# A two-layer encoder on one core: fewer, longer rotation operations on GpSimd, and new orders in the opening, the dense layer and the attention head loop

## The reference, cut to what matters

```python
mod = silu(c) @ ada_w + ada_b                      # per layer: sh1, sc1, g1, sh2, sc2, g2
# layer 0
h = modulate(rmsnorm(x, n1), sh1, sc1)
q, k, v, g = split(h @ w_in)                       # 1024, 1024, 2048, 2048 columns
q, k = axial_rope(q), axial_rope(k)                # 4 heads of 256: each half is rotated
x = x + g1 * ((silu(g) * groupnorm(retention(q, k, v))) @ w_out)
h = modulate(rmsnorm(x, n2), sh2, sc2)
x = x + g2 * ((silu(h @ w_gate) * (h @ w_up)) @ w_down)          # dense, 2816 wide
# layer 1
q, k, v = split(modulate(rmsnorm(x, n1), sh1, sc1) @ w_qkv)      # 8 heads, 2 kv heads of 128
q, k = axial_rope(rmsnorm(q)), axial_rope(rmsnorm(k))
x = x + g1 * (softmax(q k^T * scale) v @ w_out)
x = x + g2 * moe_top2_of_8(modulate(rmsnorm(x, n2), sh2, sc2))   # experts 3584 wide
out = modulate(rmsnorm(x, final_norm_g), fsh, fsc)

def rope_1d(x, pos):                               # on one half of a head
    x1, x2 = split(x, 2)
    return concat(x1 * cos - x2 * sin, x1 * sin + x2 * cos)
```

## Time and profile before

| | |
|---|---|
| median of 3 runs | 1586.56 us (1585.43 to 1588.83) |
| the profiled execution's own time | 1589.74 us |
| its span | 1587.9 us |
| instructions | 20528 |
| the chain that ended last, by engine | PE 82%, DVE 10%, ACT 3%, DMA 3%, issue 2% |
| DVE, ACT, POOL busy | 1335.5, 982.5, 198.1 us |
| HBM read | 502.12 MB, 321 GB/s over the span |

### The profile page before, as it was taken

One profiled execution on the slowest core, in us unless ns is written; L12 is line 12 of the kernel. 1 busy time (PEld: TensorE's weight loads), 2 busy tenths in 40 slices (PEclk: granted clock), 3 DMA queues, 4 the chain that ended last, 5 costly groups with the idle time before them and its releaser, 6 DMA issues.

```text
span 1587.9 us, 20528 instructions
## 1 busy us (share of the span) xinstructions
PE 1531.4 (96%) x6818; PEld 1228.9 (77%) x6818; DVE 1335.5 (84%) x1071; ACT 982.5 (62%) x811; POOL 198.1 (12%) x188
## 2 busy tenths in 40 slices
PE   6999998899999799999999999999999999999997
PEld 6777676677777588778888888888888888888885
DVE  6799878877778779998888988988988888888898
ACT  4554434343446555677777767777776777777674
POOL 0499700000020011001001001000000000000320
PEclk9999999999999999999999999999999999999999
DMA  9989735788874179999999999999999999999993
GB/s 342 380 287 350 274 105 201 272 300 298 295 249 166 46 260 344 391 346 369 375 361 367 379 358 363 386 352 365 385 353 367 381 369 352 381 369 352 390 394 141
DMA packets 238896, 508.70 MB, mean 320 GB/s; under 512 B 15494, under 2 KB 38150, under 8 KB 238728
## 3 DMA queue, kind: packets, MB, share of 16 engines
q1 hardware_dynamic: 233824, 491.52, 85.6%
q0 software_dynamic: 4448, 14.55, 2.5%
q10 hardware_dynamic: 584, 2.11, 0.3%
HBM read 502.12 MB, written 7.87 MB: 321 GB/s over the span
## 4 chain that ended last, share of the span: by engine, by line
PE 82%; DVE 10%; ACT 3%; DMA 3%; issue 2%; SPq 0%; DVEq 0%; ACTq 0%
PE bank L1969 25%; PE bank L1970 25%; PE bank L1971 25%; PE bank L2388 2%; DVE lo L1212 1%; DVE lo L1719 1%; DVE hs L1292 1%; DMA stage<-in_l_moe_w_gate 1%; PE bank L1947 1%; PE bank L2075 1%; DVE ada_acc L1224 1%; DVE lo L1609 1%; PE bank L2257 1%; ACT hi L739 0%; DMA stage<-in_l_moe_w_up 0%
## 5 line engine op out<-in xcount | busy, mean ns | idle before, releaser
L1719 DVE TENSOR_TENSOR lo<-stage,hi 128x2048 fp32r<-128x2048 f32 x168 | 388.2, 2319 | 39.6 <-ACT hi L1070 38.8
L1070 ACT CAST hi<-stage 128x2048 fp32r<-128x2048 f32 x168 | 321.3, 1914 | 107.7 <-DMA stage<-in_l_moe_w_up 86.5
L1970 PE MATMUL bank<-lo,hg_hi 128*128 128x512 f32 x896 | 353.7, 395 | 0.0
L739 ACT CAST hi<-stage 128x2048 fp32r<-128x2048 f32 x69 | 131.6, 1910 | 130.8 <-PE bank L1971 103.7
L1970 PEld LDWEIGHTS bank<-lo,hg_hi 128*128 128x128 f32 x896 | 168.9, 189 | 36.8
L1212 DVE TENSOR_TENSOR lo<-stage,hi 128x2048 fp32r<-128x2048 f32 x69 | 159.2, 2311 | 30.5 <-ACT hi L739 24.7
L1719 DVE TENSOR_TENSOR lo<-stage,hi_h 128x2048 fp32r<-128x2048 f32 x56 | 128.3, 2292 | 66.2 <-ACT hi_h L1070 66.2
L1969 PE MATMUL bank<-hi,hg_hi 128*128 128x512 f32 x452 | 178.9, 396 | 0.3 <-issue 0.2
L1971 PE MATMUL bank<-hi,hg_lo 128*128 128x512 f32 x452 | 179.0, 396 | 0.0
L1970 PE MATMUL bank<-lo,eaT_hi 128*128 128x512 f32 x448 | 177.4, 396 | 0.0
L1969 PE MATMUL bank<-hi,hT_hi 128*128 128x512 f32 x400 | 165.8, 415 | 8.5 <-DVE hT_lo L1267 3.4
(11 more groups left out here) (354 smaller groups left out, 2789.1 us busy)
## 6 DMA issues: line engine op xcount, KB each, us to landing
stage<-in_l_moe_w_gate SPq DMA_DIRECT2D x224, 512.0 KB, 5.0
stage<-in_l_moe_w_up SPq DMA_DIRECT2D x224, 512.0 KB, 5.2
stage<-in_l_moe_w_down SPq DMA_DIRECT2D x224, 512.0 KB, 4.9
ada_w<-in_l_ada_w SPq DMA_DIRECT2D x40, 1024.0 KB, 5.5
stage<-in_l_ret_w_in SPq DMA_DIRECT2D x48, 512.0 KB, 6.9
stage<-in_l_ffn_w_gate SPq DMA_DIRECT2D x22, 512.0 KB, 7.9
stage<-in_l_ffn_w_up SPq DMA_DIRECT2D x22, 512.0 KB, 8.7
stage<-in_l_ffn_w_down SPq DMA_DIRECT2D x22, 512.0 KB, 6.5
```

What stands on the lines that cost most here:

```text
L739: nc.scalar.copy(hi_of(b), stage[:, b % RING, :]).then_inc(hi_done, 1)
L1070: nc.scalar.copy(hi_e(b), stage[:, b % RING, :]).then_inc(hi_done, 1)
L1719: nc.vector.tensor_tensor(lo[:, b % RING, :], stage[:, b % RING, :], hi_e(b).bitcast(F32), ALU.subtract).then_inc(lo_done, 1)
L1970: mm(dst_ap, a_hi, w_lo, start=False, stop=False)
```

## The change

Four parts, all in the order of work or in the shape of operations; the sums that are computed stay the same.

1. **Rotation.** The loop over the two halves `f` is folded into the operands: 48 operations of 256 elements for 96 of 128.
2. **Opening.** The first unit is loaded, cast and split in two halves, each with its own semaphore, and DVE makes its `lo` ahead of `columns_pre(0)`. `low` of unit 3 moves ahead of `columns_pre(1)`.
3. **Dense layer.** SP loads a chunk's units ahead of a half of ada weights; each slot on DVE takes the second half of one ada product and the first of the next; PE's `ada_sum` comes one chunk later; `fin(6)` moves in between the first `low` and `f_mul` of the first chunk; `scale(2)` moves ahead.
4. **Attention.** The ada product A_AT-1 moves out of the head loop, ahead of and into the QKV units; its sum comes after the third turn of queries. The heads' values alternate between banks 7 and 3 (the last in 4), with `a_values(h)` waiting for `o_low` of h-2 and not h-1. In ACT's loop `soft(h+2)` comes directly behind `pT_take(h)`, the root of the second query group comes earlier with its table switched ahead (`warm[:, 5:6]`), and the last two splits of output weights (`high_o(3)`, `low_o(2)`, `low_o(3)`) move to the end of the loop.

The core of the diff:

```diff
-                    for f in range(2):
-                        co = cst[:, C_RC + (t * 2 + f) * 64:...].unsqueeze(1).to_broadcast([P, 2, 64])
-                        ...
-                        rotate(v[:, :, f, 0, :], v[:, :, f, 1, :], co, si, ("p (h i) -> p h i", dict(h=2)),
-                               [ropet[:, i, 0:128] for i in range(3)], False)
+                    co, si = (cst[:, c0 + t * 128:c0 + (t + 1) * 128].rearrange("p (f i) -> p f i", f=2).unsqueeze(1)
+                              .to_broadcast([P, 2, 2, 64]) for c0 in (C_RC, C_RS))
+                    rotate(v[:, :, :, 0, :], v[:, :, :, 1, :], co, si, ("p (h f i) -> p h f i", dict(h=2, f=2)),
+                           [ropet[:, i, :] for i in range(3)], False)
 ...
# opening, SP and ACT
-            load_in(0)
+            first = stage[:, 0, :].rearrange("p (k n) -> p k n", k=4)
+            sp.dma_start(first[:, 0:2, :], w_in_v[:, 0:2, 0:CB]).then_inc(w_first, 16)
+            sp.sem_inc(w_load[0], 16)
+            sp.dma_start(first[:, 2:4, :], w_in_v[:, 2:4, 0:CB]).then_inc(w_load[0], 16)
-            high(U_RET)
+            act.wait_ge(w_first, 16)
+            nc.scalar.copy(hi[:, 0, 0:UW // 2], stage[:, 0, 0:UW // 2]).then_inc(hi_half, 1)
+            act.wait_ge(w_load[0], 32)
+            nc.scalar.copy(hi[:, 0, UW // 2:UW], stage[:, 0, UW // 2:UW]).then_inc(hi_done, 1)
# dense, SP (load_dense: two gate/up units and one down unit)
+            load_dense(0, 0)
+            load_ada(A_FF, 0, l1_ada_w, l1_ada_b, 0)
+            load_dense(0, 1)
+            load_ada(A_FF, 1, l1_ada_w, l1_ada_b, 0)
+            load_ada(A_FF + 1, 0, l1_ada_w, l1_ada_b, AC)
# dense, DVE
+            def ada_slot(it, q):
+                ada(A_FF + q - 1, 1, it * 2)
+                ada(A_FF + q, 0, it * 2)
+            f_units(0, 0, between=lambda: fin(6))
+            fin(7)
+            ada(A_FF, 0)
+            f_units(0, 1)
+            ada_slot(0, 1)
# dense, PE
             f_down(U_FF + 4, 0, 0, True, False)
-            ada_sum(A_FF)
             f_turn(1)
-            f_chunk(U_FF + 5, 0, 2, False, A_FF + 1)
+            f_chunk(U_FF + 5, 0, 2, False, A_FF)
 ...
             f_down(U_QKV - 2, 0, N_FF - 2, False, False, between=lambda: f_turn(N_FF - 1))
+            ada_sum(A_AT - 2)
# attention, ACT
+            ada_take(A_AT - 1, mod_at((A_AT - 1 - A_L1) * AC))
+            nc.scalar.activation(warm[:, 5:6], eps, ACT.Sqrt)
+            act.wait_ge(w_used, RING + U_QKV + 6)
+            qkv_squares(2)
             qkv_copy(2)
             for h in range(AH):
                 pT_take(h)
+                if h == 0:
+                    head_roots(2)
+                if h + 2 < AH:
+                    soft(h + 2)
 ...
# attention, PE
+O_BANK = (7, 3, 7, 3, 7, 3, 7, 4)
                 pe.wait_ge(at_pT, h + 1)
-                if h:
-                    pe.wait_ge(o_lo, h)
+                if h >= 2:
+                    pe.wait_ge(o_lo, h - 1)
```

More of the change, by code:

```diff
@@ L1329, in _ @@
             pre(0, range(1, KT))
+            dve.wait_ge(hi_half, 1)
+            nc.vector.tensor_tensor(lo[:, 0, 0:UW // 2], stage[:, 0, 0:UW // 2], hi[:, 0, 0:UW // 2].bitcast(F32), ALU.subtract)
+            dve.wait_ge(hi_done, 1)
+            nc.vector.tensor_tensor(lo[:, 0, UW // 2:UW], stage[:, 0, UW // 2:UW], hi[:, 0, UW // 2:UW].bitcast(F32),
+                                    ALU.subtract).then_inc(lo_done, 1)
             columns_pre(0)
@@ L1342, in _ @@
             pre(1, range(2, 8))
+            low(U_RET + 3)
             columns_pre(1)
@@ L1346, in _ @@
                 low_pre(1, k)
-            for u in range(3, 6):
+            for u in range(4, 6):
                 low(U_RET + u)
@@ L1497, in f_low_act, with f_units @@
                                         part[:, :, :].bitcast(F32), ALU.subtract).then_inc(f_lo, 1)
-            def f_units(it, q):
+            def f_units(it, q, between=None):
                 b = U_FF + 2 + 3 * q
@@ L1503, in f_units @@
                 low(b, it * 6)
+                if between is not None:
+                    between()
                 f_mul(cc - 1)
@@ L1507, in f_units @@
                 low(b + 2, it * 6)
-            def f_pair(it):
+            def ada_slot(it, q):
[6 more added lines that the diff above has]
+            ada_slot(0, 1)
+            last = (N_FF - 1) // 2 - 1
+            with dve.Fori(1, last) as it:
                 for q in range(2):
                     f_units(it, q)
-                    for half in range(2):
-                        ada(A_FF + q, half, it * 2)
-            f_units(0, 0)
-            fin(7)
-            for half in range(2):
-                ada(A_FF, half)
-            f_units(0, 1)
-            for half in range(2):
-                ada(A_FF + 1, half)
-            last = (N_FF - 1) // 2 - 1
-            with dve.Fori(1, last) as it:
-                f_pair(it)
+                    ada_slot(it, q)
             f_units(last, 0)
-            for half in range(2):
-                ada(A_AT - 2, half)
+            ada_slot(last, 0)
+            scale(2, A_L1 + 4)
             f_units(last, 1)
-            scale(2, A_L1 + 4)
+            ada(A_AT - 2, 1)
             low(U_QKV - 1)
@@ L1551, in _ @@
                 low_T(2, (t,))
-            low(U_QKV + 2)
-            low(U_QKV + 3)
             def ada_step(c, k):
@@ L1610, in low_o @@
                                         ALU.subtract).then_inc(lo_done, 1)
+            low(U_QKV + 2)
+            for k in range(2):
+                ada_step(A_AT - 1, k)
+            low(U_QKV + 3)
+            for k in range(2, 5):
+                ada_step(A_AT - 1, k)
             link(head_rope(AH, AKV, ktab, TT))
@@ L1619, in _ @@
             low(U_QKV + 5)
+            for k in range(5, KT):
+                ada_step(A_AT - 1, k)
             head_rope(0, 2, qtab, 2 * TT).then_inc(arope, 1)
@@ L2291, in _ @@
             aq_turn(2)
+            ada_sum(A_AT - 1)
             qkv_half(5, 0)
```

98 lines of the change are left out of this document (40 added, 58 removed).

## The result

The change makes the kernel slower by 0.4%: 1593.82 us in the median of 6 runs (1591.74 to 1596.06) against 1586.44 of the kernel before (6 runs on the same chip), ratio 1.0041, 95% interval 1.0028 to 1.0053 (the ratio compares all runs and is not the quotient of the two medians, 1.0047). The forecast was 1572.6. The profiled execution took 1593.38 us with a span of 1591.6. GpSimd is busy for 163.9 us in place of 198.1, as the shorter list of operations says, but the chain that ended last is now 77% TensorE and 14% VectorE, from 82 and 10.

A forecast was written before the change was run, and what follows sets the result against it. TensorE's matmuls, its waits and the half-clock stretches behind them bound the kernel. Rotation 0.2, opening 4.5, dense layer 5.3 and 0.7, attention 3.3 sum to 14.0 us: from 1586.6 to 1572.6 us, range 1566.5 to 1581.

The forecast's parts named there:

- For twice the length, 0.2: Input product: VectorE's ada step, delayed 0.1 us beside 128-element GpSimd operations, would be delayed 0.2 us by twice the length.
- rival (a): Input product: longer GpSimd operations hold up VectorE; 0 to 0.5 us, at worst 1607 us; chance 0.04 beyond 0.36 us.
- The rotation's gain: TensorE's first turn: its weight load no longer waits for the rotation's end; 0.2 us, 0 to 0.46.
- Its length: GpSimd's rotation by 48 operations of 256 elements takes 75 us, with bounds of 36 and 122.
- Opening, 4.5 us forecast: Kernel start: earlier first product and unit 3 without its wait, less one slow clock stretch; 4.5 us, 4.3 to 6.1.
- marks of the mechanism: Opening: first low part at 26.3 us, TensorE's second sum at 43.7, unit 3 near 48.4 without a wait for `lo`.
- one stretch of 1.55 us: Opening: TensorE's standstill ahead of the second sum brings back one half-clock stretch costing 1.55 us.
- Dense layer, 5.3 and 0.7: Dense layer: 5.3 us from the second chunk's wait and clock (2.5 to 6.1), 0.7 at the layer's end (0 to 0.9).
- The first chunk's product: Dense layer: with `fin(6)` moved in, the first chunk's product step ends at 280.35 us, not ahead of 279.88.
- Attention, 3.3: Attention: vanished waits less new ones give 2.3 us, plus 1 us of clock; 3.3 us, bounds 0 and 6.5.
- my 8.0: Attention: new TensorE waits at query turns and in the head loop, 8.0 us in all.
- rival (b): New waits and the clock eat the gain: attention 0, dense 2.5, opening 4.3, in all 7 us, 1579.6 us; chance 0.20.

The follow-up runs named there:

- e11: Kernel after with all 8 gate operations held until the last gate columns are there: 1588.81 us, ratio 1.0011 against before.
- e2: Kernel before with only the new rotation, 48 operations of 256 elements: 1602.97 us, ratio 1.0093 against before.
- e3: Kernel after with each of the 8 gate operations of 512 elements cut into four of 128: 1587.82 us, ratio 0.9998 against before.
- e1: Kernel after with the old rotation, 96 operations of 128 elements: 1577.37 us, ratio 0.9929 against before.
- e4: Kernel after with the rotation left out, queries and keys unrotated: 1578.21 us, ratio 0.9936 against before.
- e5: Kernel before with the new opening alone: 1585.23 us, ratio 0.9995 against before.
- e8: Kernel after with the old rotation and three ada steps of the attention moved behind the first two query pairs' rotations: 1575.86 us, ratio 0.9933 against before.
- e10: Kernel after with the old rotation, the same kernel as e1 run once more: 1578.76 us, ratio 0.9940 against before.
- e12: Kernel after with half the rotation, by 96 operations of 64 elements, the other half unrotated: 1579.84 us in a single run.
- e6: Kernel before with the new dense layer alone: 1584.41 us, ratio 0.9986 against before.
- e7: Kernel before with the new order in the attention alone: 1583.46 us, ratio 0.9979 against before.
- e9: Kernel before with the new dense layer and new attention, old opening and old rotation: 1582.32 us, ratio 0.9969 against before.
- e13: e1 with 26 dummy matmuls in TensorE's wait ahead of the opening's second sum: ratio 0.9944 against before.
- e16: e1 with 13, 8, 7 and 5 dummy matmuls in four TensorE waits, in the opening and ahead of three turns: 1575.38 us, ratio 0.9926 against before.

## Why the prediction was wrong

**Rotation: the step that failed.** The sign that I had named for being wrong, a wait of TensorE in the input product, is what the profile shows. "For twice the length, 0.2" was the error: I took VectorE's delay as proportional to the length of GpSimd's operation. By the runs a step takes 0.76 us beside operations of 64 elements, 0.85 of 128, 1.13 of 256 and 1.66 to 1.83 of 512. Against GpSimd's times alone (0.454, 0.76 by the fit, 1.377 for 512 in e11) the additions are 0.1, 0.38 and about 1.0: in each case the operation's whole time less 0.35 to 0.38 us (0.76 is a fit, no 256-element operation was seen alone). The excess over that free part counts, and it grows fourfold from 128 to 256. My formula for rival (a), with x = 1.13 - 0.85 = 0.28, gives 6.4 x (8 x 0.28 - 0.16) - 3.5 = 9.8 us; e2 is 9.9 late at the first turn. So mechanism and sum of the rival were there, and its price and its chance (0.04) were wrong. What I cited from the Trainium skill (SBUF: State Buffer, Who interferes with whom) fits better than I allowed: the later one does wait for the earlier, except for some 0.36 us of each GpSimd operation, which made 0.1 of 0.454 look like almost nothing.

**The gates were missing in every case.** I moved the rotation's end to before 145 us and did not ask what GpSimd does next. From the first to the third turn the kernel after needs 5.3 us more, and e3 and e11 both take that away. 3.74 of it is the wait for `dec`, and the rest is the half clock behind it, from 194.0 to 197.5 us. With the rotation's 10 us that makes 15. The runs have 14.8 us (e2 against before) and 17.9 (the kernel after against e1, 1.0041 / 0.9929).

**The rotation's gain** of 0.2 us: e1 and e4 can't be told apart, so there was none to be had. Its length: 75 us forecast, 67.7 busy.

**Opening, 4.5 us forecast.** In six profiles with the new opening and VectorE not held up (e1, e4, e5, e8, e10, e12) the first turn lies 1.6 to 4.3 us ahead, 2.9 in the mean; in four without it (with before, e6, e7, e9) it lies from 1.4 us behind to 1.3 ahead, 0.1 ahead in the mean. All marks of the mechanism are right (26.3, 43.7, no wait ahead of unit 3). The clock was mis-sized: I gave one stretch of 1.55 us back, and the traces have one to three in a row, from 46 us to 49 in e1, from 44 to 51 in the kernel after, from 43 to 53 in e12, and none in e3. The four kernels with dummies have none, so it is most likely the standing still ahead of the sum that brings them. What the part is worth in the median stays open between 0.8 us (e5, -1.3 to 2.7) and 3.6 (e9 beside e10).

**Dense layer, 5.3 and 0.7.** Between the first and the third turn every kernel with the new order is 4.9 or 6.4 us shorter than before (36.8 or 38.3 us in place of 43.19; the longer ones have a half-clock stretch just behind the first turn, such as 278.0 to 281.5 us in e1). The first chunk's product was right, the clock at 1.00 behind it too. The 0.7 us at the layer's end did not come: from its last turn to the attention's first turn it is 0.4 us longer (11.14 to 10.69), for the added sum lies on the path and lets nothing go earlier. Measured alone the layer is worth 2.2 us (0.5 to 3.8) against my 6.0, less than the marks too. 1 us of the difference is that 43.19 is high: e5 and e7, with the old layer, need 42.1 us there, with one half-clock stretch and not two. The rest isn't accounted for.

**Attention, 3.3.** Measured alone 3.3 (1.4 to 5.4). The waits for `prob` are gone, and 6.0 us at three query turns and 1.8 for `aqT` stand in their place (e7), close to my 8.0. Behind it, on the way to the experts, nothing is shown to be lost: from router to experts the kernels of the table with the new attention need 119.3 to 124.7 us, those with the old one 119.7 to 121.7.

All three together gave 0.9929 and 0.9940, or 9.5 to 11.3 us in place of the 13.8 forecast for them.

**Slips in the sums.** 3.4 + 2.7 - 0.86 is 5.2 and not 5.3, the waits in the attention leave 10.2 - 8.0 = 2.2 and not 2.3, rival (b) left out the 0.7 us of the layer's end (7.7 us, 1578.9), and unit 3's row gives 7.5 us and not 7.45. None of them bears on the miss.

## What to carry to other kernels

Ahead of making GpSimd's operations longer, look what VectorE does beside them: what counted here is how far each one's time alone lies over a free part (0.36 us), times their number. Many short operations cost GpSimd, which had time; few long ones cost VectorE, which had none. And when an engine off the path gets done earlier, follow what it starts next and beside whom.

## What the runs showed of the hardware that I had not expected

GpSimd operations of 64 elements (0.32 us at the shortest) leave a VectorE operation of 0.75 us all but unchanged (0.761). It is mostly GpSimd that pays: in e12 an operation that meets a subtract takes 2.37 us, the one ahead of it 0.32, and the subtract 2.47 in place of 2.29 (timeline, GpSimd, then VectorE):

```profile
90.67 0.32 POOL L635 TENSOR_TENSOR ropet<-proj,cst 128x64 f32<-128x64 f32 x1
90.95 2.37 POOL L636 TENSOR_TENSOR proj<-proj,cst 128x64 f32<-128x64 f32 x1
...
90.67 2.47 DVE L1234 TENSOR_TENSOR lo<-stage,hi 128x2048 fp32r<-128x2048 f32 x1
```

Cutting the gates from 8 operations to 32 raised GpSimd's time from 15.0 to 29.2 us and made the kernel faster. And dummy matmuls in a wait of 3.4 us kept the granted clock at 1.00 in the stretch behind it in each of the four kernels that had them (e13 to e16); without them eight of nine kernels had a stretch at 0.50 there.
